# A gate table built from one-hot products: the gate moves to the other factor, and VectorE writes its four one-hot rows in one compare

## The reference, cut to what matters

```python
def peer_ffn(x, wq, keys, u, v):
    ...
        best_s, best_pos = lax.top_k(cand_s.reshape(c, PEER_HEADS, -1), PEER_TOPK)
        idx = jnp.take_along_axis(cand_i.reshape(c, PEER_HEADS, -1), best_pos, axis=-1)
        gate = jax.nn.softmax(best_s, axis=-1)
        ue = u[idx]
        ve = v[idx]
        act = jax.nn.gelu(jnp.einsum('td,thkd->thk', xc, ue).astype(jnp.float32), approximate=False)
        return jnp.einsum('thk,thkd->td', (gate * act).astype(xc.dtype), ve)
```

## Time and profile before

| | us |
|---|---|
| median of three runs | 2989.59 (2984.39 to 2993.38) |
| the profiled execution | 2979.47 |
| its span | 2977.8 |
| TensorE busy in the span | 2846.4 |
| VectorE busy | 1781.1 |
| ScalarE busy | 920.1 |
| GpSimd busy | 330.5 |
| the two stages that make the gate table | 1331.5 to 1424.5 and 2362.0 to 2455.3 from the span's start |

### The profile page before, as it was taken

How to read it: one execution, slowest core, us unless ns; L and a number is a source line. 1 busy time by engine, 2 the same in 40 slices (tenths; PEclk the granted TensorE clock), 3 DMA queues, 4 the chain that set the end, 5 groups by cost and what they waited for, 6 DMA issues and landing times.

```text
span 2977.8 us, 46537 instructions
## 1 busy us (share of the span) xinstructions
PE 2846.4 (96%) x17164; PEld 2591.0 (87%) x17164; DVE 1781.1 (60%) x4030; ACT 920.1 (31%) x1939; POOL 330.5 (11%) x397
## 2 busy tenths in 40 slices
PE   8999999999998999999999899989999999999998
PEld 5888888779887888999998899978889999998998
DVE  6888888556666876879333333268678793333432
ACT  4222322334764664126111000046631351110000
POOL 0000000000000000029111111000000381111100
PEclk9999999999999999999999999999999999999999
DMA  7333333223223333783687788523447746877983
GB/s 292 115 123 114 123 114 114 85 80 138 86 86 114 111 131 129 264 314 129 239 296 287 279 334 330 207 99 114 143 133 294 266 143 255 299 295 274 346 318 116
DMA packets 101184, 575.32 MB, mean 193 GB/s; under 512 B 9072, under 2 KB 9456, under 8 KB 52144
## 3 DMA queue, kind: packets, MB, share of 16 engines
q1 hardware_dynamic: 79936, 420.23, 39.6%
q0 software_dynamic: 21104, 153.23, 13.4%
HBM read 572.38 MB, written 1.05 MB: 193 GB/s over the span
## 4 chain that ended last, share of the span: by engine, by line
PE 82%; DMA 7%; DVE 5%; issue 2%; ACT 2%; DVEq 1%; ACTq 0%; POOL 0%; SPq 0%; POOLq 0%
PE bank L2516 19%; PE bank L2457 11%; PE bank L494 10%; PE bank L496 9%; PE bank L495 9%; PE bank L2505 7%; DMA wring<-in_w_peer 7%; PE bank L2490 2%; PE bank L1676 2%; PE bank L2477 2%; PE bank L997 1%; PE bank L986 1%; PE bank L1370 1%; PE bank L1388 1%; DVE arena L2796 1%
## 5 line engine op out<-in xcount | busy, mean ns | idle before, releaser
L2516 PE MATMUL bank<-arena,wring 128*128 128x192 f32 x4096 | 683.1, 326 | 0.3 <-DMA wring<-in_w_peer 0.3
L2516 PEld LDWEIGHTS bank<-arena,wring 128*128 128x128 f32 x4096 | 668.7, 190 | 2.3 <-issue 2.3
L478 DVE TENSOR_TENSOR peer_r<-wring,peer_r 128x512 fp32r<-128x512 f32 x440 | 296.2, 697 | 215.2 <-ACT peer_r L473 212.2
L494 PE MATMUL bank<-h_r,peer_r 128*128 128x512 f32 (+1 forms) x1088 | 397.0, 365 | 5.4 <-DVE h_r L508 3.3
L496 PE MATMUL bank<-h_r,peer_r 128*128 128x512 f32 (+1 forms) x1088 | 384.2, 353 | 0.0
L2571 POOL DMA_INDIRECT arena<-in_experts,arena x128 | 154.6, 1208 | 1873.6 <-DVE arena L2773 1011.6
L2505 PE MATMUL bank<-res,wring 128*128 128x192 f32 x1664 | 298.3, 334 | 44.5 <-DMA wring<-in_w_peer 44.0
L473 ACT ACTIVATE peer_r<-wring 128x512 fp32r<-128x512 f32 x440 | 266.6, 628 | 231.3 <-PE bank L496 227.8
L495 PE MATMUL bank<-h_r,peer_r 128*128 128x512 f32 (+1 forms) x960 | 333.7, 348 | 0.0
L2505 PEld LDWEIGHTS bank<-res,wring 128*128 128x128 f32 x1664 | 273.7, 192 | 61.8 <-issue 37.8
L2457 PE MATMUL bank<-res,wring 128*128 128x192 f32 x1920 | 313.1, 326 | 0.0
(11 more groups left out here) (403 smaller groups left out, 4118.1 us busy)
## 6 DMA issues: line engine op xcount, KB each, us to landing
wring<-in_w_peer SPq DMA_DIRECT2D x256, 1024.0 KB, 5.6
wring<-in_w_proj SPq DMA_DIRECT2D x34, 1024.0 KB, 4.8
wring<-in_w_hy SPq DMA_DIRECT2D x32, 1024.0 KB, 5.1
arena<-in_w_ada POOLq DMA_DIRECT2D x16, 1024.0 KB, 5.1
wring<-in_w_out SPq DMA_DIRECT2D x16, 1024.0 KB, 4.8
wring<-in_w_ada SPq DMA_DIRECT2D x8, 1024.0 KB, 10.1
wring<-in_w_hyout SPq DMA_DIRECT2D x8, 1024.0 KB, 4.9
wring<-in_w_q SPq DMA_DIRECT2D x8, 1024.0 KB, 4.8
```

What stands on the lines that cost most here:

```text
L478: v.tensor_tensor(SPLIT[:, buf, 1, :], raw_quarter(name, i, j, q), SPLIT[:, buf, 0, :].bitcast(F32), ALU.subtract).then_inc(split_lo, 1)
L494: pe.matmul(out_ap, w_hi, x_hi, start=start, stop=False, **kw)
L2516: mm = pe.matmul(expert_sum(k), wring[:, s, at + k * P:at + (k + 1) * P], GP[:, par, :], start=False, stop=True, skip_group_check=True)
```

## The change

The gate no longer multiplies `OHA` but `OHB`. `OHA` becomes a pure compare, so VectorE makes a group's four rows in one tensor_tensor over 128 x 512: `iota` repeated four times against four numbers of plane 1, each repeated over 128 columns. The row of `OHB` that VectorE makes and the rows that GpSimd makes are multiplied by the gate in the same instruction (is_equal and mult, now with two numbers of a partition). ScalarE needs gate - gate x |iota - index| instead of 1 - |iota - index|, so its second instruction takes the gate as its bias and the negated gate as its scale. The negated gate is a new plane 3 of `PAIR`, made ahead of `pair_ready` by a drain and one more ScalarE instruction over 128 x 256.

```diff
@@ the planes (L291)
-        PAIR = c5.take(3, T)
+        PAIR = c5.take(4, T)
@@ peer_scalar
-                a = act.activation(PAIR[:, :, tt * P:(tt + 1) * P], view(bank[2 + tt][:, 0:3 * P], 3), ACT.Copy)
-            a.then_inc(pair_ready, 1)
+                act.activation(PAIR[:, 0:3, tt * P:(tt + 1) * P], view(bank[2 + tt][:, 0:3 * P], 3), ACT.Copy)
+            act.drain()
+            act.activation(PAIR[:, 3, :], PAIR[:, 0, :], ACT.Copy, scale=-1.0).then_inc(pair_ready, 1)
             act.drain()
@@ hots_scalar
-                act.activation(OHB[:, t, :], NEAR[:, n % 2, :], ACT.Relu, scale=-1.0, bias=ones[:, 0:1]).then_inc(hot_c, 1)
+                act.activation(OHB[:, t, :], NEAR[:, n % 2, :], ACT.Relu, scale=pair[:, 3, n // 2, t, :],
+                               bias=pair[:, 0, n // 2, t, :]).then_inc(hot_c, 1)
@@ peer_pool
-                    a = pool.tensor_scalar(OHB[:, 4 * (n % 2) + s, :], iota, pair[:, 2, n // 2, 4 * (n % 2) + s, :], None,
-                                           ALU.is_equal)
+                    a = pool.tensor_scalar(OHB[:, 4 * (n % 2) + s, :], iota, pair[:, 2, n // 2, 4 * (n % 2) + s, :],
+                                           pair[:, 0, n // 2, 4 * (n % 2) + s, :], ALU.is_equal, ALU.mult)
@@ hots (VectorE)
                 if par:
                     t = 4 * par
-                    v.tensor_scalar(OHB[:, t, :], iota, pair[:, 2, n // 2, t, :], None, ALU.is_equal)
-                for s in range(4):
-                    t = 4 * par + s
-                    a = v.tensor_scalar(OHA[:, t, :], iota, pair[:, 1, n // 2, t, :],
-                                        pair[:, 0, n // 2, t, :], ALU.is_equal, ALU.mult)
-                a.then_inc(hot, 1)
+                    v.tensor_scalar(OHB[:, t, :], iota, pair[:, 2, n // 2, t, :], pair[:, 0, n // 2, t, :], ALU.is_equal,
+                                    ALU.mult)
+                four = slice(4 * par, 4 * par + 4)
+                v.tensor_tensor(OHA[:, four, :], wide(iota, 1, 4), pair[:, 1, n // 2, four, :].to_broadcast([P, 4, P]),
+                                ALU.is_equal).then_inc(hot, 1)
```

## The result

The changed kernel takes 3040.44 us (median of 4 runs, 3036.24 to 3050.39) against 2991.49 of the kernel before beside it. The ratio is 1.0163, with a 95% interval of 1.0118 to 1.0209: 35 to 63 us slower. The profiled execution took 3050.39 us and is the longest of the four, so the two traces are compared by stage and not by span.

A forecast was written before the change was run, and what follows sets the result against it. TensorE bounds the kernel now; GpSimd, needing 103.0 us, would lengthen each table stage from 93.0 to 105.2. With 0.6 ahead, 2 x (12.2 + 0.6) = 25.6, say 26, on 2989.6 gives 3015.6 us, range 2998 to 3044.

The forecast's parts named there:

- The bound and the direction: Gate-table stages: GpSimd, with 5.5 us of room, becomes the bound; stage 105.2 us instead of 93.0; slower, chance 0.81.
- VectorE's gain: VectorE in the table stages: saves 25 us a layer, at the very best 6.4 us of it on the path.
- The stop by two inputs from SBUF: GpSimd's compares stand still until VectorE's tensor_tensor ends, then need 0.47 us; 0.31 us each, 14.9 us a layer.
- The rival in which repeated operands don't stop GpSimd: VectorE's tensor_tensor leaves GpSimd unstopped; time within -4 to about +5 us; part of the within-0.3% outcome, chance 0.15.
- The second number on GpSimd's compare: GpSimd's OHB compares: a second number adds 0.055 us to each of 120, 6.6 us a layer.
- the second number is dear: Rival: the second number costs each GpSimd compare 0.15 to 0.32 us, giving 3040 to 3080; chance 0.11.
- The small terms: New plane and drain 0.6 us a layer ahead of the stage; ScalarE's changed second instruction costs nothing that shows.
- Relief of GpSimd: Rival: replacing VectorE's four tensor_scalar compares frees GpSimd, at most 2.3 us a layer; 2978 us; chance 0.04.

The follow-up runs named there:

- shared rows, PSUM: Changed kernel with the index read from PSUM and GpSimd making 72 OHB rows a layer, not 120; 2982.22 us against 2985.43 before, ratio 0.9991.
- the version with 72 compares: Changed kernel, index still from SBUF, with OHB rows shared out anew so GpSimd makes 72 a layer, not 120; 2995.33 us, ratio 1.0033.
- the short compares: Kernel before with OHA's four rows in one tensor_tensor reading SBUF, no gate in the table, GpSimd's compare with one number; 3009.03 us, ratio 1.0061.
- the two versions that read PSUM: Tensor_tensor index from PSUM: kernel before with four rows in one and no gate, ratio 1.0017; changed kernel with its gate, ratio 1.0104.
- the constant: Changed kernel, but GpSimd multiplies its compare by a constant instead of a second number per partition; 3038.57 us, ratio 1.0171.
- one-number compares of VectorE: Changed kernel, but VectorE makes its four OHA rows in four one-number tensor_scalar compares, no tensor_tensor; 3029.52 us, ratio 1.0130.
- the best version: Changed kernel with index from PSUM, 72 GpSimd rows, earlier pair_ready, split gather step and GpSimd's gather issue two groups later; 2986.99 us, ratio 0.9984.
- four rows from PSUM: Kernel before with OHA's four rows in one tensor_tensor reading its indices from PSUM, no gate in the table; 2989.26 us, ratio 1.0017.
- the issue moved as well: Same run as the best version: GpSimd's gather issue moved two groups later, on top of the split gather step; 2986.99 us, ratio 0.9984.

## Why the prediction came out as it did

- **The bound and the direction** held. GpSimd had 5.5 us of room in the stage and became its bound; taking work from it (shared rows, PSUM) took the whole loss away. VectorE's gain was off the path.
- **The stop by two inputs from SBUF** held in kind. The prediction took 0.31 us for each tensor_tensor; in the changed kernel it is 0.31, in the version with 72 compares 0.40, with the short compares 0.39. That the 0.31 was met is in part luck. It came from taking off 15 of 48 tensor_tensors that would find GpSimd idle, and none does: all 96 of the two stages catch a compare, which then takes 1.12 us on average. Without that discount the working gives 0.38 here and 0.41 for the short compares. Nor is the phase random, as it assumed, since all makers start from one event. The compares end 0.66 us behind the tensor_tensor (93 of the 96), not 0.47. With the short compares it is 0.47 (82 of 96), so the 0.20 us of the second operation lie almost wholly behind the reading. The rival in which repeated operands don't stop GpSimd is out.
- **The second number on GpSimd's compare is the term that was mis-sized.** I took 0.055 us from VectorE's own second number; GpSimd's compare went from 0.585 to 0.785 start to start. Between the two versions that read PSUM, without and with the gate, its compares grow from 76.9 to 100.1 us, 0.19 each. With 0.20 the prediction's own sum gives 81.5 + 24 + 14.9 + 2.2 = 122.6 us for the stage; the trace shows 123.2. It was also misnamed: the constant costs as much as the number, so the price is the second operation's. The rival "the second number is dear", 0.15 to 0.32 at 3040 to 3080, is the case that came true, at its edge, and I had given it 0.11. The measured median of 3040.4 lies within the range, near its upper end, where the prediction's point was 3015.6. With 0.20 in its sum the prediction would have said 2 x (29.6 + 0.6) = 60 us, 3050 for a median, which is outside the range. The median came out 10 us lower for a reason that no run shows, so that the range held is luck in part.
- **Why the nearest row misled.** VectorE's second number costs it at most 0.09 us; GpSimd's costs more than twice that. The row on GpSimd itself, its tensor_tensor at 2.5 ns a column, gave 0.32 for a second pass over 128 columns. The truth, 0.20, lies midway between the two. What went wrong is that I took a little over half of the smaller one, and let the range end at 0.15, when a row of the engine itself stood at 0.32.
- **The small terms.** ScalarE's new plane put the start back by some 0.5 us, as reckoned with 0.6. Its second instruction grew from 402 to 494 ns and cost nothing that shows. VectorE's tensor_tensor was 727 ns on average where 697 was expected, for now it sometimes waits for GpSimd in turn: 8 of the 96 take 1.03 us, and each of these starts 0.06 us behind the start of a compare. It is 682 where it reads PSUM, and none is over 0.69 there. VectorE's busy time in the stage fell by 18 us where 25 were expected, which changes nothing off the path.
- **Relief of GpSimd**, the rival on the other side, is out for this kernel. The Trainium skill's sentence behind it ("SBUF — State Buffer", "Who interferes with whom", on tensor_scalar in a two-port mode) is borne out in a weak form at most: beside one-number compares of VectorE GpSimd's busy time is 110.8 us of the stage, and with the tensor_tensor from PSUM in their place 104.1. No run shows whether a port mode is the reason. By that page of the Trainium skill the ports go to whichever instruction issues first, so GpSimd need not be the one that stands, as the prediction had read it. The other half of what that page of the Trainium skill states, that a tensor_tensor with two SBUF inputs contends with GpSimd's reads and one with a single SBUF input does not, is just what the PSUM runs show: 121 of the changed kernel's 240 compares are over 0.05 us longer than the shortest, and 23 with the index from PSUM, 16 of them under gather steps.
- **What remains open.** The two stages of the profiled executions grew by 60 us together and the rest of the span by 11, the median by 49 with an interval up to 63. And the best version's shorter waits did not shorten its stages in full; TensorE's busy time in them rose from 85.8 to 87.1 and 88.6 us. The second of these stages was granted 0.98 of the clock, which accounts for some of it; the first was granted 1.00.

## What to carry to other kernels

Read slack in the stage, engine by engine: an engine that is busy for 11% of the program can be at 89% of the stage that matters, and an edit that relieves its neighbour may still load it. On VectorE count, beside an instruction's length, how many of its inputs lie in SBUF while GpSimd works; moving one input to PSUM freed GpSimd at no cost that shows here. Where a new operation has no row, and a row of another engine and a far row of the same one enclose it, let the range reach from one to the other and put the point between them. When the second half of a step is moved, move with it what waits for it in another engine's queue.

## What was not expected of the hardware

**A second operation costs GpSimd 0.20 us** in a compare over 128 x 128, whether its operand is a number per partition or a constant, and the constant's compares are recorded 0.07 us shorter at the same step from start to start.

**The clock at the stage's start.** In the changed kernel TensorE idles for 4.41 us ahead of the first group (2.62 before): 0.5 of the added 1.8 us is the new plane, the rest GpSimd's three compares of that group. It then runs at about half the clock. TensorE in order of time and the stretch's granted clock (the last but two of the numbers):

```profile
1337.67 2.04 PE L2490 MATMUL bank<-arena 128*128 128x128 f32 x8 [4.41 <-POOL arena L2682]
```
```profile
1337.90:1342.30 4.40, 4.40 (x20) 4.40 (x21) 1.10 (x2) 1.18 (x3) 3.71 (x5) 0.51 0.00 0
```

0.51 is the lower of the two levels, 1.2 GHz; it was 1.00, 2.4 GHz, in the kernel before at this place. The same stretch of records took 1.13 us before and 2.04 now. The length of the idle stretch does not settle it alone. Of the 22 stages traced in this case (11 kernels, two each), all ten that start with TensorE idle for 3.4 to 4.4 us have the lower level in their first groups, and seven of the twelve with 2.4 to 2.7 us. In three versions one stage had it and the other did not: 92.8 us, granted 0.98, against 90.4, granted 1.00 (shared rows, index from PSUM; 2.48 us of idle ahead of both); 93.3 against 91.7 (four rows from PSUM); 91.3 against 90.1 (the issue moved as well). Compared in this way the lower clock costs a stage that TensorE bounds 1.2 to 2.4 us, as much as some of the differences between these versions.
